# One 4 MB load for the four down units of a job, in the mixture-of-experts stage of a decoder layer

## What is computed

```python
def moe(h, router_w, router_b, w_gate_up, b_gate_up, w_down, b_down):
    top_v, top_i = lax.top_k(h @ router_w + router_b, TOP_K)   # 4 of 32 experts for each of 512 tokens
    gates = jax.nn.softmax(top_v, axis=-1)
    ...
    def expert_block(args):
        xblk, e = args                                  # rows of one expert
        act = clamped_swiglu(xblk @ w_gate_up[e] + b_gate_up[e])   # 1024 x 2048
        return act @ w_down[e] + b_down[e]                         # 1024 x 1024
    ...
x = x + moe(rmsnorm(x, norm2_g))
return rmsnorm(x, final_g)
```

## Time and profile before

| | |
|---|---|
| median of 3 runs | 1308.74 us (1307.56 to 1310.19) |
| the profiled execution's own time | 1309.16 us |
| its span | 1307.3 us |
| TensorE busy | 1179.6 us, 90% of the span |
| VectorE, ScalarE, GpSimd busy | 525.0, 178.0, 229.2 us |
| moved by DMA | 455.47 MB |

### The profile page before, as it was taken

The page is one execution under the profiler, slowest core; times in us unless marked ns, Lnnn a source line. Parts: engine busy times, 40 slices in busy tenths (PEclk is TensorE's granted clock), DMA queues, the critical chain, the costliest instruction groups (busy, mean ns, idle before and its releaser), DMA issues.

```text
span 1307.3 us, 24934 instructions
## 1 busy us (share of the span) xinstructions
PE 1179.6 (90%) x8884; PEld 444.1 (34%) x8885; DVE 525.0 (40%) x1643; ACT 178.0 (14%) x331; POOL 229.2 (18%) x233
## 2 busy tenths in 40 slices
PE   7998998995999989999999997879999798987886
PEld 5743554451323323333333232223332232322222
DVE  2002332244545434444444343334444343443356
ACT  2112333210110101111111110001110010100011
POOL 0054433001211111111111111111111111111110
PEclk9999999996999999999999998889999899998999
DMA  9422201047899999999999999999999999999998
GB/s 374 192 100 80 81 33 65 17 177 277 325 425 427 426 422 426 425 426 423 426 425 425 426 424 425 424 425 424 425 425 427 424 426 426 425 424 425 425 420 322
DMA packets 45955, 455.47 MB, mean 348 GB/s; under 512 B 7961, under 2 KB 9333, under 8 KB 20076
## 3 DMA queue, kind: packets, MB, share of 16 engines
q1 hardware_dynamic: 34876, 430.62, 78.6%
q0 software_dynamic: 9568, 22.30, 4.6%
q10 hardware_dynamic: 1488, 2.25, 0.5%
HBM read 444.65 MB, written 16.81 MB: 353 GB/s over the span
## 4 chain that ended last, share of the span: by engine, by line
PE 63%; DMA 27%; DVE 4%; issue 3%; POOL 2%; ACT 1%; SPq 0%; POOLq 0%; DVEq 0%; ACTq 0%
PE bank L774 33%; DMA arena<-in_w_gate_up 21%; PE bank L802 11%; PE bank L550 6%; PE bank L624 3%; PE bank L568 3%; PE bank L793 3%; DMA arena<-y_rows 2%; DMA arena<-in_w_down 2%; PE bank L611 1%; PE bank L583 1%; PE bank L597 1%; DMA h_rows<-arena 1%; PE bank L753 1%; DMA y_rows<-hT,arena 1%
## 5 line engine op out<-in xcount | busy, mean ns | idle before, releaser
L774 PE MATMUL bank<-arena,hT 128*32 128x512 f32 x5120 | 578.5, 605 | 37.0 <-DMA arena<-in_w_gate_up 30.5
L774 PEld LDWEIGHTS bank<-arena,hT 128*32 128x32 f32 x5120 | 160.1, 111 | 423.9 <-issue 378.8
L802 PE MATMUL bank<-arena,hT 128*64 128x512 f32 x1024 | 246.7, 638 | 48.1 <-DVE hT L1395 48.1
L802 PEld LDWEIGHTS bank<-arena,hT 128*64 128x64 f32 x1024 | 75.3, 146 | 212.4 <-issue 144.4
L1088 POOL DMA_INDIRECT hT<-h_rows,arena x82 | 83.5, 1019 | 294.9 <-issue 161.8
L991 ACT ACT_TABLE_LOAD x48 | 61.6, 1283 | 521.1 <-DVE hT L1373 520.8
L1383 DVE TENSOR_TENSOR arena<-bank,gain 128x512 f32<-128x512 f32 x80 | 55.4, 692 | 163.8 <-PE bank L774 163.8
L1111 POOL DMA_INDIRECT y_rows<-hT,arena x32 | 32.7, 1022 | 424.8 <-DVEq L1411 206.4
L550 PE MATMUL bank<-hT,arena 128*128 128x512 f32 x224 | 102.2, 604 | 0.0
L991 ACT ACTIVATE arena<-arena 128x256 f32<-128x256 f32 x80 | 33.3, 416 | 342.7 <-DVE arena L1385 342.7
L1413 DVE TENSOR_TENSOR hT<-bank,gain 128x512 f32<-128x512 f32 x32 | 22.1, 692 | 133.0 <-PE bank L802 132.6
(11 more groups left out here) (169 smaller groups left out, 754.5 us busy)
## 6 DMA issues: line engine op xcount, KB each, us to landing
arena<-in_w_gate_up SPq DMA_DIRECT2D x128, 2048.0 KB, 25.7
arena<-in_w_down SPq DMA_DIRECT2D x64, 2048.0 KB, 21.3
arena<-in_w_in SPq DMA_DIRECT2D x10, 1024.0 KB, 16.0
arena<-y_rows SPq DMA_DIRECT2D x3, 2048.0 KB, 26.5
arena<-in_w_out SPq DMA_DIRECT2D x4, 1024.0 KB, 15.4
arena<-bias_by_dist POOLq DMA_DIRECT2D x6, 512.0 KB, 4.1
xs<-in_x SPq DMA_DIRECT2D x4, 512.0 KB, 8.3
h_rows<-arena POOLq DMA_DIRECT2D x4, 512.0 KB, 2.9
```

The source lines that it names most:

```text
L774: mm = pe.matmul(bank[c][j * CH:(j + 1) * CH, :].rearrange("p (g n) -> p g n", g=2), xT[:, c, k * CH:(k + 1) * CH], w[:, :, j * Q:(j + 1) ...
L802: mm = pe.matmul(bank[3][g * 2 * CH:(g + 1) * 2 * CH, :], aT_pair[:, k].rearrange("p c s -> p (c s)"), w[:, g * 2 * Q:(g + 1) * 2 * Q], st ...
```

## The change

Gate units stay loads of two. The four down units of a job become one load: 32 KB in a partition, 4 MB, with one semaphore of its own, `downs_full`. SP issues it once `dn_done` says that the job ahead has read its downs; the wait on `units_used` for units 8 and 9 is gone. Before its first down matmul of a job TensorE waits for the whole load, where it waited for units 8 and 9 first and for units 10 and 11 half way. At the start the one load of job 0 is issued at `op_done`, and nothing at `out_used`.

```diff
-            sp.wait_ge(out_used, 2)
-            load_two(0, 8, 0)
+            def load_downs(e):
+
+                src = w_down[bass.ds(e, 1)].rearrange("e (p k) n -> (e p) (k n)", p=P)
+                sp.dma_start(ring[:, KT:JOB_UNITS, :].rearrange("p u n -> p (u n)"), src).then_inc(downs_full, 16)
+
             sp.wait_ge(op_done, TT)
-            load_two(0, 10, 0)
+            load_downs(0)
...
+            def load_late(e, job, half, free_of, low):
+
+                load_part(e, job, half, range(HALF, KT, 2), free_of, low)
+                sp.wait_ge(dn_done, low + AHEAD)
+                sp.sem_inc(waited_sp, 1)
+                sp.wait_ge(downs_full, job * 16)
+                sp.sem_inc(waited_sp, 1)
+                load_downs(e)
...
-                    load_part(expert(job), job, 1 - half, late, pair * 2 + half, counted(job))
+                    load_late(expert(job), job, 1 - half, pair * 2 + half, counted(job))
...
                 with pe.If(chunks > 2):
                     pe.wait_ge(act_done, low + (AHEAD - 2))
+                    pe.wait_ge(downs_full, full)
                     for k in range(KT):
-                        if k % 4 == 0:
-                            pe.wait_ge(two_full[(KT + k // 2) // 2], full)
                         down_third(k)
                 pe.wait_ge(act_done, low + AHEAD)
+                pe.wait_ge(downs_full, full)
                 for k in range(KT):
-                    if k % 4 == 0:
-                        pe.wait_ge(two_full[(KT + k // 2) // 2], full)
                     down_pair(k)
```

More of the change, by code:

```diff
@@ L300, in program @@
         mix_full = [sem(f"mix_full{s}") for s in range(MIX_RING)]
-        two_full = [sem(f"two_full{u}") for u in range(0, JOB_UNITS, 2)]
+        two_full = [sem(f"two_full{u}") for u in range(0, KT, 2)]
+        downs_full = sem("downs_full")
         units_used = sem("units_used")
@@ L408, in wait_read @@
                     sp.wait_ge(gu_done, low + AHEAD)
-                elif u + 2 == JOB_UNITS:
-                    sp.wait_ge(dn_done, low + AHEAD)
                 else:
-                    sp.wait_ge(units_used, job * FREED + (u + 2 - (u >= KT)))
+                    sp.wait_ge(units_used, job * FREED + u + 2)
             def load_two(e, u, half):
[L415 to L418, removed]
+                src = w_gate_up[bass.ds(e, 1)].rearrange("e (p m k) n -> (e m) p (k n)", p=P, k=2)[u // 2]
                 a = ring_slot(half, u)
@@ L456, in expert @@
                 return sp.value_load(jobs_i[0:1, 0, bass.ds(job, 1)], min_val=0, max_val=E - 1)
-            ahead, rest, late = range(0, EARLY, 2), range(EARLY, HALF, 2), range(HALF, JOB_UNITS, 2)
+            ahead, rest = range(0, EARLY, 2), range(EARLY, HALF, 2)
             more = sp.value_load(njobs_i[0:1, 2:3], min_val=E // 2 - 1, max_val=JOBS_MAX // 2 - 2)
@@ L474, in _ @@
             job = fewer * 2 + 2
-            load_part(expert(job), job, 0, late, fewer * 2 + 1, counted(job))
+            load_late(expert(job), job, 0, fewer * 2 + 1, counted(job))
             load_part(expert(fewer * 2 + 3), fewer * 2 + 3, 1, range(0, HALF, 2), fewer * 2 + 1)
@@ L490, in read_rank @@
                     .then_inc(ranks_in[k], 16)
-            load_part(expert(last), last, 1, late, more * 2, counted(last))
+            load_late(expert(last), last, 1, more * 2, counted(last))
             sp.wait_ge(scattered, jobs_before(3) * 32 + 32)
```

## The result

| | before | changed |
|---|---|---|
| median of 7 runs each | 1308.74 us (1305.97 to 1310.19) | 1316.43 us (1311.41 to 1319.02) |
| ratio, 95% interval | | 1.0055 [1.0043, 1.0067] |
| the profiled execution, its span | 1309.16 us, 1307.3 us | 1319.02 us, 1316.9 us |

By the ratio of the runs the changed kernel is 0.55% slower, 7.2 us (5.6 to 8.8); the two medians lie 7.7 us apart. 5.8 us was forecast, and 1314.5 us. The profiled execution is the longest of its seven, 2.6 us above the median, so its single times are read with that much caution, and where it matters the profiles of the other kernels stand beside it.

The account below looks back on a forecast made before the run. DMA, full with weights from 346 to 1288 us, was taken as the bound. 3.5 + 2.0 + 0.7 + 2.0 - 2.4 = 5.8 us gave 1314.5 us, 0.44% slower, range 1307.0 to 1321.0.

Parts of the forecast that it names:

- mechanism A: The forecast itself: losses mainly at both ends, where the queue is not full, sum 5.8 us, 1309.4 to 1320.7; chance 60%.
- job 1, +3.5: Start: job 1's down 8 issued 3.45 us later on a dry queue, a delay that stays to the end; +3.5 us.
- the dry stretch near the end, +0.7: Job 30's load: job 29's stall of 2.8 us exceeds the 2.1 us left queued, so DMA runs dry; +0.7 us.
- Job 0's downs, +2.0: Start: later down 8 is in flight beside the store and gathers, delaying the store and the last gather; +2.0 us.
- The forecast's own sign of being wrong: Mid-stretch: the forecast counts as wrong if DMA's share drops below 1 there.
- TensorE's waits in the full stretch, 0: Mid-stretch: waiting for all four units makes gaps in 18 jobs, 26.6 us together, hidden by shorter gate waits; 0 us.
- The end, +2.0: Jobs 30 and 31 run 2.8 us later and so do the last rank's reads; +2.0 us, bounds 0.8 and 2.8.
- Packets, -2.4: Down loads: packets of 32 KB for 16 KB save 256 per engine, at most 14 ns each; -2.4 us.
- B: Rival: faster by larger packets, the down bytes' rate up by 3% or more, 1304 us with 4%; chance 8%.
- C: Rival: no measurable change, store's delay and end mostly hidden, packets give 3 us, 1310 us; chance 20%.
- D: Rival: TensorE's waits for whole downs add up and DMA runs dry in mid-stretch, up to 1338 us; chance 10%.
- E: Rival: a fixed 2.3 us saved for each of 32 loads fewer, 74 us, 1235 us; chance 2%.

Follow-up runs that it names:

- e3: Changed kernel, but each job's downs come by two 2 MB loads at the late place and TensorE waits for halves as before: 1.0046.
- e2: Changed kernel, but each 4 MB down load is two loads of 2 MB at the same late place; TensorE waits for the whole: 1.0069.
- e12: Changed kernel with job 1's downs alone loaded as before, a second time, beside the changed kernel on the same occasion: 1316.32 us, 1.0067.
- e11: The changed kernel itself, unaltered, measured again on another occasion: 1314.98 us, 1.0057.
- e1: Changed kernel, but job 0's downs come by two loads at their old places: 1314.73 us, 1.0042.
- e5: Changed kernel with the downs of jobs 0 and 1 loaded as before; TensorE waits for whole downs in every job: 1.0027.
- e9: Changed kernel with job 1's downs alone loaded as before, first time: 1.0050.
- e7: Changed kernel, but the downs of jobs 29 to 31 are loaded as before; TensorE still waits for whole downs: 1.0039.
- e6: Changed kernel with 4 MB down loads for jobs 2 to 28 alone; other jobs load as before, and there TensorE waits for halves: 0.9995.
- e4: Changed kernel with loads and their issue as before the change; TensorE waits for both halves before its first down matmul: 0.9993.
- e8: As e6, and gate units 0 to 3 of jobs 3 to 29 also come by one load of 32 KB per partition: 1307.19 us, 0.9983.
- e10: The kernel of e8 measured a second time on another occasion: 1307.05 us, 0.9988.

## Why the prediction was right, and where it was not

The direction and the size held: +7.2 us for +5.8, with mechanism A, a loss at places where the queue is dry. That the sum comes so near is in part luck. One term was too large as it stood (job 1, +3.5, worth 0 to 2 us here) and one too small (the dry stretch near the end, +0.7, worth 2 to 4). The late issue alone costs 6.0 us (e3), and in this there is not only what the forecast had at the start, 3.5 + 2.0, but also a dry stretch near the end.

*Job 0's downs, +2.0.* Right in size. From the store's issue to the first gate matmul it takes 17.9 to 18.4 us in the seven profiles with down 8 at its old place (mean 18.13) and 19.7 to 20.0 in the seven with the late load (mean 19.85): +1.7 us. The way to it was not as forecast. The store was not slowed at all, and not only the last gather meets the end of the bulk: all three do, the first most (5.7 us for 3.0). Wrong is the hint at the packets: the Trainium skill's rule that an engine changes queues at packet boundaries (DMA: Bandwidth & Descriptors, "Queues, rings and completion order") spoke for more delay behind packets of 32 KB, and with 16 KB (e2, e3) the same path takes 20.0 us, no less. The runs don't contradict the rule; they show that here it decides nothing, since the gathers land when the bulk is through.

*Down 8 of job 1, "this stays to the end", +3.5.* The first half is right: the load goes out at 348.76, the share before it falls to 0.37, and in e12 against e11 the next loads are 3.0 us better off. The second half holds only up to 1225 us, by the sums of bytes. "DMA is full from there on" failed: between 1225 and 1250 us it runs dry, and for longer where it is further ahead. By the times, undoing job 1 is worth 2.0 us with job 0 also as before (e1 1.0042, e5 1.0027; not told from nothing) and nothing with job 0 late (e9, e12). Where the end is not dry, as in e7, the start keeps its price: e7 less e6 is 5.8 us, for the 3.5 + 2.0 of the forecast. A delay at the start is thus partly a loan from a later point. The forecast's own sign of being wrong, a share below 1 in mid-stretch, also came, but small: 0.97 from 700 to 710 and from 720 to 730 us in the profiled execution. Over 710 to 740 us the rate is 414 GB/s for 427 before, 0.9 us of DMA; e11 and e12 don't differ there (415 and 414), and e3 shows no such dip (425), so job 1's gain is not lost there.

*The dry stretch after job 29, +0.7.* Right place, too small. The share over 1225 to 1250 us falls from 1.01 to 0.83 in the profiled execution and to 0.91 in e11: (425 - 340) x 25 = 2.1 MB and (425 - 376) x 25 = 1.2 MB, at 425 GB/s 5.0 and 2.9 us of DMA. The step that failed is the cover. The forecast set job 29's own stall of 2.8 us against the 2.1 us that are left queued at that issue. But the load of job 30 goes out at 1239.03, 8.6 us later than down 10 did (1230.4), while the loads ahead of it are through some 3 us later (near 1235.4, by the rates of single microseconds, for the forecast's 1230.4 + 2.1). TensorE had fallen behind step by step: the downs of job 28 start 5.4 us later than before and those of job 29 7.9 us, of which 2.7 are job 0's later start. In each of these two jobs it waits for its downs (5.5 us for 3.0), and its matmuls then take 9.5 us for 8.8. To this comes the time before a load's first byte: 0.5 to 0.9 us, an estimate from what DMA moved in the single microseconds after the issues at 348.76 and 1239.03. e3, in which the wait for downs is as before, is dry there as well (360 GB/s): there the load goes out at 1235.13, 4.7 us later than before.

*TensorE's waits in the full stretch, 0.* Right: e4 has 12 of them ahead of `down_pair`, the longest 2.9 us above the 3.00 that were there anyway (forecast: 18 jobs, the longest 2.8), and costs nothing. In the changed kernel the waits of TensorE's matmuls for gates fell in return, from 30.5 to 12.1 us.

*The end, +2.0.* Not settled. In the profiled execution the last down load lands at 1283.6, 7.7 us later than before, and the last rank's reads go out 11.4 us later (the forecast said 6 or so), the span is 9.6 longer: some 2 us lie behind the last load. e4, which has the same wait, shows none in its times. Between 0 and 2.

*Packets, -2.4.* Right in direction, the size is not settled. 10 to 13 ns a packet by the queues' rows (forecast 14 as a ceiling), but 6 to 18 with their rounding; 1.7 us by the times of e2, not told from nothing, and nothing to be seen in e6; e8 and e10, which are told from nothing, speak for 3 to 5 ns a packet, some 1 us here. The rate where the queue is full is 425 to 426 GB/s in the changed kernel, for 425.

*Rivals.* B falls: at most 0.5% more rate (427 for 425, in e8), not 3%. C came true for no kernel with the late start. D falls by e4. E falls: 32 loads fewer, and nothing like 74 us; the fixed 2 us that the Trainium skill gives for a DMA issued from GpSimd (DMA: Bandwidth & Descriptors, "Anatomy of one DMA") are there around a single load from SP (2.3 us) and are not paid in a full queue. The same page's "Rules for kernel authors" would coalesce many small transfers; these were of 2 MB already, and joining them further is worth 0.1 to 0.2% here (e8, e10), and only for loads that are not made later by it.

Of the down loads' times to landing, forecast at 20 to 25 us, the median is 19.8 and the shortest 13.5. Two kernels that differ in one thing differ also by chance: the store of job 0 is issued anywhere between 290.6 and 295.4 us in the profiles, whatever the kernel, so one span against another tells 2 us at best.

## What to carry to other kernels

Joining two loads makes the first as late as the second. Price that at the issue where the queue is shallowest: the time to landing, less that of the same load on an empty queue, less the bytes that the change takes out ahead of it. Then ask how late the issue comes there against DMA's own lateness, with all stalls of the jobs before added up, not the last one alone; with some 2 us left DMA ran dry here for 3 to 5 us, and the larger packets (0.1%) don't pay for it. Join loads that could be issued together anyhow, as the gate loads of e8. And before a delay at the start is said to stay to the end, look for a point further on where the queue runs dry anyway, for there it is partly given back.

## What the runs showed that I had not expected

- A gather of 32 rows takes 2.5 to 3.0 us on an empty DMA. Behind bulk it lands when the bulk is through, here after 5.7 to 6.5 us for the first of three; a store of 512 KB ahead of it takes 10.7 to 11.4 us in either case, and packets of 16 or of 32 KB in the bulk make no difference that shows.
- After a wait of 5 us TensorE's next 32 down matmuls take 9.5 us. The granted clock over the 7 us from 1283 on is 0.59 in the profiled execution:

```profile
1283.00:1290.00 7.00, 6.22 (x18) 2.14 (x20) 0.27 (x2) 0.00 (x0) 1.02 (x1) 0.59 1.02 403
```

  By single microseconds TensorE is idle from 1278.8 to 1283.8 us, and the granted clock goes from 1.00 to 0.50, the lower of its two levels (1.2 GHz), at about 1282; it is back at 1.00 at 1289. In the kernel before the wait was 3.00 us: the clock stayed at 1.00 through job 31's matmuls (7.09 us) and was 0.76 over the 7 us from 1221 on, in job 29 (8.78 us). So waits for DMA that are hidden otherwise can make the work behind them slower too. It costs where TensorE is on the path, at the last job, and where it sets the time of a late load, as at 1236 us above.
